# Dilated attention: relative bias added in PSUM by identity matmuls, exp read from PSUM

## Chip, cores and metric

The kernel runs on all 8 cores of one Trainium2 chip, one program on each. The time is device microseconds of the slowest core.

## What is computed

One decoder layer over 16384 positions of width 1024: forgetting attention (8 heads), dilated sliding-window attention (8 heads of 64), a cross-attention to 256 memory positions and a SwiGLU network. The part that matters here is the dilated attention. For each of three patterns (window, dilation), and within each residue class, a block of 128 queries sees its own block of 128 keys and the one before:

```python
DILATED_PATTERNS = ((128, 1), (512, 4), (2048, 16))
s = einsum('bhrnqd,bhrnkd->bhrnqk', qs, kk) * Dh ** -0.5      # blocks: 128 queries, 2 x 128 keys
s = s + bias                                                 # T5 bucket of the distance, per head
s = where(band & not_first, s, -inf)
o = softmax(s) @ vv ; lse = log of the denominator
# the three patterns are mixed with softmax(lse)
```

## The kernel before

Each core owns 2048 positions. It works in four stages with barriers between them: projections of the whole sequence (lines 395 to 497), forgetting attention (652 to 690), dilated attention (from 739), and everything after the attention (from 918). A small tracker records every instruction with the buffers that it reads and writes, in program order; each engine's queue is that order, and the waits are worked out from the buffers.

The dilated stage goes head by head. `c_loads(h)` loads Q, K, V and two bias tables of a head from HBM, on SyncE's queue (SP), into one of two sets; it is called a head ahead. BIC is 3 tables of 128 keys x 512 (the same 128 columns four times), for the current block, BIP 3 tables of 128 x 128 for the previous block; both hold -30000 where the band ends. Then V is transposed by TensorE in nine groups of up to 8 tiles (L854), each copied to VD by VectorE (L857); there is one PSUM bank for it, so matmuls and copies alternate. VD has ones in its columns 64 to 127, so that P.V yields the denominator too.

Twelve batches follow, four for each dilation 1, 4, 16. A batch is four items (query block, its key block, the previous key block). K, Q as matmul operands have 64 rows (head dimension); for d = 4 and d = 16 they are read in strides of 4 and 16 elements. A batch has three steps:

- s1: eight matmuls of 64 rows and 128 columns: four (L791) into one PSUM bank Sc_ps, four (L794) into another, Sp_ps
- s23: VectorE adds the tables, one L798 for Sc_ps and four L807 for Sp_ps, or L803 where the item reaches into the halo before the core's own positions and the mask HMASK is added too; ScalarE takes the exp of each (L809, L810)
- s45: eight matmuls of 128 rows and 128 columns (L815 and L817 in turn) multiply with VD into OD_ps; VectorE copies (L829) or adds (L831) that into ACCD

Sc_ps, Sp_ps and OD_ps have two banks each. The order is written out: s1 and s23 of the first two batches, then for each batch i its s45 followed by s1 and s23 of batch i + 2. A head ends with a reciprocal of the denominators (L871) and a multiply (L872), both on VectorE.

Of the kernel before, what the change touches and what calls it, by code (L numbers as in the profile page):

```python
# [6 lines left out]
F32 = mybir.dt.float32  # L7
BF16 = mybir.dt.bfloat16
AF = mybir.ActivationFunctionType
ALU = mybir.AluOpType  # L10
# [212 lines left out]
def build_program(debug=False):  # L223
    nc = bass.Bass("TRN2", target_bir_lowering=False)
    mk = MK(nc)
# [62 lines left out]
    with ExitStack() as st:  # L288
        ARENA_F = 49 * 1024
        arena_t = st.enter_context(nc.sbuf_tensor("arena", [128, ARENA_F], F32))  # L290
        ar = Arena(arena_t, ARENA_F)
# [3 lines left out]
        def B(name):  # L295
            return mk.buf(name)
# [4 lines left out]
        IDB = ar.alloc(128, BF16)  # L301
# [3 lines left out]
        HMASK = ar.alloc(1, F32)  # L305
# [3 lines left out]
        bC = B("consts")  # L309
# [7 lines left out]
        bC2 = B("consts2")  # L317
# [4 lines left out]
                                         op0=ALU.mult), reads=[bC], writes=[bC, bC2])  # L322
# [13 lines left out]
        for i in range(7):  # L336
            s = i % 2
            mk.dma(lambda e, i=i, s=s: e.dma_start(out=WST[s], in_=w_a_v[:, :, 440 * i:440 * (i + 1)]),
                   writes=[bWST[s]])
            for kc in range(8):  # L340
                if kc % 2 == 0:
                    mk.dve(lambda e, i=i, s=s, kc=kc: e.tensor_scalar(out=WA[:, kc, 440 * i:440 * (i + 1)], in0=WST[s][:, kc, :],
                                                                      scalar1=GPRE[:, 0, kc:kc + 1], scalar2=None, op0=ALU.mult),
                           reads=[bWST[s], bC], writes=[bWAc[i]])
                else:
                    mk.act(lambda e, i=i, s=s, kc=kc: e.activation(out=WA[:, kc, 440 * i:440 * (i + 1)], in_=WST[s][:, kc, :],
                                                                   func=AF.Copy, scale=GPRE[:, 0, kc:kc + 1]),
                           reads=[bWST[s], bC], writes=[bWAc[i]])
# [96 lines left out]
        for b in range(NBLK):  # L445
# [21 lines left out]
            for i in range(4):  # L467
# [3 lines left out]
                       reads=[bPR[k]], writes=[bVT[vs]])  # L471
# [4 lines left out]
            if b % 2 == 1:  # L476
                sb_ = b // 2
                mk.dma(lambda e, sb_=sb_: e.dma_start(out=V_v[:, :, 1024 * sb_:1024 * (sb_ + 1)],
                                                      in_=VST.rearrange("p h t d -> p h (t d)")),
                       reads=[bVST], writes=[DB("V", sb_)], eng="act")  # L480
            mk.act(lambda e, k=k: e.activation(out=GE[0:8, :], in_=PR_ps[k][0:8, :], func=AF.Exp,
                                               bias=NBF[0:8, :], scale=-1.0), reads=[bPR[k], bC2], writes=[bGE])
            mk.act(lambda e: e.activation(out=GSP[0:8, :], in_=GE[0:8, :], func=AF.Ln, bias=1.0, scale=1.0),
                   reads=[bGE], writes=[bGSP])
            cs = b % 2
            if b == 0:
                mk.dve(lambda e: e.tensor_tensor_scan(out=CS[0][0:8, :], data0=ONES8[0:8, :], data1=GSP[0:8, :],
                                                      initial=0.0, op0=ALU.mult, op1=ALU.add),
                       reads=[bGSP, bC2], writes=[bCS[0]])
            else:  # L490
                mk.dve(lambda e, cs=cs: e.tensor_tensor_scan(out=CS[cs][0:8, :], data0=ONES8[0:8, :],
                                                             data1=GSP[0:8, :], initial=CS[1 - cs][0:8, 511:512],
                                                             op0=ALU.mult, op1=ALU.add),
                       reads=[bGSP, bC2, bCS[1 - cs]], writes=[bCS[cs]])
            if b >= 28:
                ob = b - 28
                mk.dve(lambda e, cs=cs: e.tensor_scalar(out=NCS[0:8, :], in0=CS[cs][0:8, :], scalar1=-1.0, scalar2=None,
                                                        op0=ALU.mult), reads=[bCS[cs]], writes=[bNCS])
                mk.dma(lambda e, ob=ob: e.dma_start(out=C_s[:, 512 * ob:512 * (ob + 1)], in_=NCS[0:8, :]),
                       reads=[bNCS], writes=[DB("C", ob)], eng="act")  # L500
# [197 lines left out]
        for h in range(8):  # L698
            for ci in range(4):
                ulist = [(kt, p) for kt in range(32 * ci, 32 * ci + 32) for p in range(2) if kt <= last_kt(2 * p + 1)]  # L700
                units = {}
                n = len(ulist)
# [17 lines left out]
        DQT2 = [ar.alloc(OWN, BF16) for _ in range(2)]; bDQT2 = [B("DQT0"), B("DQT1")]  # L720
        DKT2 = [ar.alloc(2 * OWN, BF16) for _ in range(2)]; bDKT2 = [B("DKT0"), B("DKT1")]
        DVT2 = [ar.alloc(2 * OWN, BF16) for _ in range(2)]; bDVT2 = [B("DVT0"), B("DVT1")]
        BIC2 = [ar.alloc(3 * 512, F32).rearrange("p (b n) -> p b n", n=512) for _ in range(2)]; bBIC2 = [B("BIC0"), B("BIC1")]
        BIP2 = [ar.alloc(3 * 128, F32).rearrange("p (b n) -> p b n", n=128) for _ in range(2)]; bBIP2 = [B("BIP0"), B("BIP1")]
        VD = ar.alloc(69 * 128, BF16).rearrange("p (t d) -> p t d", d=128)
        bVD = B("VD")
        SC2 = [ar.alloc(512, F32) for _ in range(2)]; bSC2 = [B("SC0"), B("SC1")]
        SPv2 = [ar.alloc(512, F32) for _ in range(2)]; bSPv2 = [B("SPv0"), B("SPv1")]
        PC2 = [ar.alloc(512, BF16) for _ in range(2)]; bPC2 = [B("PC0"), B("PC1")]
        PP2 = [ar.alloc(512, BF16) for _ in range(2)]; bPP2 = [B("PP0"), B("PP1")]  # L730
        ACCD = ar.alloc(OWN, F32); bACCD = B("ACCD")
# [26 lines left out]
        def c_loads(h):  # L758
            z = h % 2
            mk.dma(lambda e: e.dma_start(out=DQT2[z][0:64, :], in_=DQ_s[h]), reads=allDQ, writes=[bDQT2[z]])  # L760
            mk.dma(lambda e: e.dma_start(out=DKT2[z][0:64, :], in_=DK_s[h]), reads=allDK, writes=[bDKT2[z]])
            mk.dma(lambda e: e.dma_start(out=DVT2[z][0:64, :], in_=DV_s[h]), reads=allDV, writes=[bDVT2[z]])
            mk.dma(lambda e: e.dma_start(out=BIC2[z], in_=dbiasc_d[h].rearrange("b p n -> p b n")), writes=[bBIC2[z]])
            mk.dma(lambda e: e.dma_start(out=BIP2[z], in_=dbiasp_d[h].rearrange("b p n -> p b n")), writes=[bBIP2[z]])

        def make_batch(h, bi, d, g, vidx):
            z = h % 2
            DQT, DKT, BIC, BIP = DQT2[z], DKT2[z], BIC2[z], BIP2[z]
            bDQT, bDKT, bBIC, bBIP = bDQT2[z], bDKT2[z], bBIC2[z], bBIP2[z]
            KV = kview(DKT[0:64, :], d)  # L770
            QV = qview(DQT[0:64, :], d)
            y = cst["n"] % 2
            cst["n"] += 1
            Sc_ps, bScp, Sp_ps, bSpp, OD_ps, bODp = Sc_ps2[y], bScp2[y], Sp_ps2[y], bSpp2[y], OD_ps2[y], bODp2[y]
            SC, bSC, SPv, bSPv, PC, bPC, PP, bPP = SC2[y], bSC2[y], SPv2[y], bSPv2[y], PC2[y], bPC2[y], PP2[y], bPP2[y]
            items = []
            for jj in range(4):
                if d == 1:
                    j = 4 * g + jj
                    items.append((QV[:, j, :], KV[:, 16 + j, :], KV[:, 15 + j, :], vidx[(1, 16 + j)], vidx[(1, 15 + j)], j == 0))  # L780
                elif d == 4:
                    m, r = g, jj
                    items.append((QV[:, m, r, :], KV[:, 4 + m, r, :], KV[:, 3 + m, r, :], vidx[(4, 4 + m, r)],
                                  vidx[(4, 3 + m, r)], m == 0))
                else:
                    r = 4 * g + jj
                    items.append((QV[:, r, :], KV[:, 1, r, :], KV[:, 0, r, :], vidx[(16, 1, r)], vidx[(16, 0, r)], True))

            def s1():
                for jj, it in enumerate(items):  # L790
                    mk.pe(lambda e, jj=jj, it=it: e.matmul(Sc_ps[:, 128 * jj:128 * (jj + 1)], it[1], it[0], start=True, stop=True),  # L791
                          reads=[bDKT, bDQT], writes=[bScp])
                for jj, it in enumerate(items):
                    mk.pe(lambda e, jj=jj, it=it: e.matmul(Sp_ps[:, 128 * jj:128 * (jj + 1)], it[2], it[0], start=True, stop=True),  # L794
                          reads=[bDKT, bDQT], writes=[bSpp])

            def s23():
                mk.dve(lambda e: e.tensor_tensor(out=SC, in0=Sc_ps, in1=BIC[:, bi, :], op=ALU.add),  # L798
                       reads=[bScp, bBIC], writes=[bSC])
                for jj, it in enumerate(items):  # L800
                    sl_ = slice(128 * jj, 128 * (jj + 1))
                    if it[5]:
                        mk.dve(lambda e, sl_=sl_: e.scalar_tensor_tensor(out=SPv[:, sl_], in0=Sp_ps[:, sl_], scalar=HMASK[:, 0:1],  # L803
                                                                        in1=BIP[:, bi, :], op0=ALU.add, op1=ALU.add),
                               reads=[bSpp, bBIP, bC], writes=[bSPv])
                    else:
                        mk.dve(lambda e, sl_=sl_: e.tensor_tensor(out=SPv[:, sl_], in0=Sp_ps[:, sl_], in1=BIP[:, bi, :], op=ALU.add),  # L807
                               reads=[bSpp, bBIP], writes=[bSPv])
                mk.act(lambda e: e.activation(out=PC, in_=SC, func=AF.Exp), reads=[bSC], writes=[bPC])  # L809
                mk.act(lambda e: e.activation(out=PP, in_=SPv, func=AF.Exp), reads=[bSPv], writes=[bPP])  # L810

            def s45():
                for jj, it in enumerate(items):
                    sl_ = slice(128 * jj, 128 * (jj + 1))
                    mk.pe(lambda e, sl_=sl_, it=it: e.matmul(OD_ps[:, sl_], VD[:, it[3], :], PC[:, sl_], start=True, stop=False),  # L815
                          reads=[bVD, bPC], writes=[bODp])
                    mk.pe(lambda e, sl_=sl_, it=it: e.matmul(OD_ps[:, sl_], VD[:, it[4], :], PP[:, sl_], start=False, stop=True),  # L817
                          reads=[bVD, bPP], writes=[bODp])
                if d == 1:
                    oap = ACCD[:, 512 * g:512 * (g + 1)]  # L820
                    iap = OD_ps[:, :]
                elif d == 4:
                    oap = ACCD[:, 512 * g:512 * (g + 1)].rearrange("p (i r) -> p r i", r=4)
                    iap = OD_ps[:, :].rearrange("p (r i) -> p r i", r=4)
                else:
                    oap = ACCD[:, :].rearrange("p (i r) -> p r i", r=16)[:, 4 * g:4 * g + 4, :]
                    iap = OD_ps[:, :].rearrange("p (r i) -> p r i", r=4)
                if d == 1:
                    mk.dve(lambda e: e.tensor_copy(out=oap, in_=iap), reads=[bODp], writes=[bACCD])  # L829
                else:  # L830
                    mk.dve(lambda e: e.tensor_tensor(out=oap, in0=oap, in1=iap, op=ALU.add), reads=[bODp, bACCD], writes=[bACCD])  # L831
            return (s1, s23, s45)

        c_loads(0)
        for h in range(8):
            z = h % 2
# [408 lines left out]
```

How the kernel before makes its waits and increments, by code:

```python
                def body(eng):  # L168
# [2 lines left out]
                    def wait(sem, val):  # L171
                        kid = id(sem)
                        if known.get(kid, 0) >= val:
                            return
                        known[kid] = val
                        eng.wait_ge(sem, val)
# [10 lines left out]
                                wait(d.key.sem, d.key.inc_amt * dv)  # L187
                            else:
                                wait(esem[d.eng][d.sigval[0]], d.sigval[1])
                        ins = o.fn(eng)
                        if o.is_dma:
                            ins.then_inc(o.key.sem, o.key.inc_amt)
                        elif o.needs_signal:
                            ins.then_inc(esem[o.eng][o.sigval[0]], 1)
                    if ename == "sp":
                        for (k, v) in fin:
                            eng.wait_ge(k.sem, v)
```

## Time and profile before

| | |
|---|---|
| runs shown | 4790.36 and 4900.81 us, median 4845.58 us |
| the profiled execution | 4801.83 us, span of its slowest core (core 3) 4799.6 us |
| spans of the 8 cores | 4758.5 to 4799.6 us |
| busy, share of the span | TensorE (PE) 78%, weight loads (PEld) 31%, VectorE (DVE) 27%, ScalarE (ACT) 58%, GpSimd (POOL) 12% |
| mean granted TensorE clock, core 3 | 0.883 |

A profile comes from one execution and shows its slowest core. A busy time is the sum of an engine's instructions; matmuls overlap one another, so the distance from one start to the next tells their rate, not the duration of one. PEclk is the share of the full TensorE clock of 2.4 GHz that was granted. In a timeline, neighbours of the same line and shape are merged into one row with their count; a PE row is matmuls, a PEld row weight loads. An arrow with a name tells what an engine waited for.

### The profile page before, as it was taken

The page shows a single profiled execution, that of the slowest core. Times are in us where ns is not written, and L with a number is a line of the kernel's source. Part 1 is how long each engine was busy: PE and PEld are TensorE (multiplying, and loading weights), DVE is VectorE, ACT ScalarE, POOL GpSimd, SP SyncE. Part 2 cuts the span into 40 slices and gives each one's busy share as a digit, 9 for nine tenths or more (in the row PEclk, how much of TensorE's full clock was granted, in tenths as well). Part 3 has the DMA queues.
Part 4 walks back from the last instruction along what each step waited for, and adds up shares of the span by engine and source line. Part 5 has one row for each costly group of instructions (what it writes and reads, how often), then busy time and mean ns, then how long its engine had stood idle before and what let it go on. Part 6 is the DMA issues. An engine that isn't in the chain of part 4 may idle for free.

```text
span 4799.6 us, 63084 instructions; the slowest of 8 cores (4758.5 to 4799.6 us)
## 1 busy us (share of the span) xinstructions
PE 3751.5 (78%) x16856; PEld 1487.3 (31%) x16856; DVE 1281.0 (27%) x1945; ACT 2799.0 (58%) x3379; POOL 578.5 (12%) x509
## 2 busy tenths in 40 slices
PE   1787888892999999999999999995555437676767
PEld 0333333331333333333333333333333213232333
DVE  1332331114101020111111111007778432333321
ACT  2222222231999999999999999992222235353521
POOL 2333332200010002011120303200000000000000
PEclk9998999996999999999999999995555559898988
DMA  5455453222021112122221312202110302524245
GB/s 169 138 157 147 125 162 110 93 85 76 28 76 29 48 29 68 45 63 64 60 82 47 95 34 82 86 1 58 39 39 20 106 0 75 159 77 160 75 157 163
DMA packets 236377, 399.33 MB, mean 83 GB/s; under 512 B 16712, under 2 KB 110152, under 8 KB 228840
## 3 DMA queue, kind: packets, MB, share of 16 engines
q1 hardware_dynamic: 187072, 332.30, 23.2%
q10 hardware_dynamic: 48960, 63.00, 4.0%
q8 instruction: 147, 2.41, 0.2%
q14 instruction: 198, 1.62, 0.1%
HBM read 302.37 MB, written 92.86 MB: 82 GB/s over the span
## 4 chain that ended last, share of the span: by engine, by line
PE 51%; ACT 21%; DVE 12%; DMA 8%; issue 6%; ACTq 1%; SPq 0%; POOL 0%; DVEq 0%; POOLq 0%
PE psall L652 15%; ACT arena L667 14%; PE psall L677 11%; PE psall L395 10%; DMA KT_s<-arena 4%; PE psall L1131 2%; PE psall L1116 2%; DVE arena L871 2%; PE psall L1111 2%; ACT arena L935 2%; PE psall L1037 1%; DVE arena L960 1%; DVE arena L688 1%; ACT arena L810 1%; DVE arena L803 1%
## 5 line engine op out<-in xcount | busy, mean ns | idle before, releaser
L667 ACT ACTIVATE arena<-psall,arena 128x1024 bf16<-128x1024 f32 (+1 forms) x1984 | 1988.9, 1102 | 167.9 <-PE psall L652 155.1
L652 PE MATMUL psall<-arena 128*128 128x512 bf16 x3904 | 1172.2, 378 | 139.7 <-DVE arena L628 86.9
L677 PE MATMUL psall<-arena 128*128 128x512 bf16 x3904 | 1168.3, 379 | 29.0 <-DVE arena L690 15.6
L395 PE MATMUL psall<-arena 128*128 128x512 bf16 (+1 forms) x3072 | 729.9, 395 | 18.0 <-ACT arena L403 18.0
L652 PEld LDWEIGHTS psall<-arena 128*128 128x128 bf16 x3904 | 264.3, 96 | 995.9 <-issue 967.8
L677 PEld LDWEIGHTS psall<-arena 128*128 128x128 bf16 x3904 | 372.6, 96 | 516.4 <-issue 68.2
L688 DVE RECIPROCAL arena<-psall 64x512 f32<-64x512 f32 x32 | 107.5, 3359 | 1271.4 <-PE psall L677 1271.2
L395 PEld LDWEIGHTS psall<-arena 128*128 128x128 bf16 (+1 forms) x3072 | 299.1, 100 | 386.4 <-issue 75.1
L403 ACT ACTIVATE arena<-psall 128x512 bf16<-128x512 f32 x224 | 133.7, 597 | 332.3 <-PE psall L395 251.7
L599 POOL TENSOR_SCALAR arena<-arena 128x128 bf16<-128x128 f32 x352 | 212.0, 602 | 571.8 <-DMA arena<-w_gate 271.0
L809 ACT ACTIVATE arena<-arena 128x512 bf16<-128x512 f32 x96 | 60.7, 632 | 319.6 <-PE psall L794 240.0
L470 ACT ACTIVATE arena<-psall 128x512 bf16<-128x512 f32 x128 | 74.6, 597 | 274.3 <-PE psall L459 154.5
L416 POOL TENSOR_TENSOR arena<-arena 128x4096 bf16<-128x4096 f32 x32 | 224.4, 7013 | 68.8 <-DMA arena<-xT 68.8
L1131 PE MATMUL psall<-arena 128*128 128x512 bf16 x704 | 165.4, 392 | 71.9 <-DMA arena<-Wd_b 65.2
L1111 PE MATMUL psall<-arena 128*128 128x512 bf16 x704 | 179.7, 401 | 49.6 <-DMA arena<-Wg_b 48.3
L425 DVE TENSOR_TENSOR arena<-arena 128x512 bf16<-128x512 f32 x192 | 132.9, 692 | 291.1 <-PE psall L395 97.1
L935 ACT ACTIVATE arena<-psall 128x512 bf16<-128x512 f32 x96 | 57.4, 598 | 247.0 <-PE psall L1131 92.0
L1116 PE MATMUL psall<-arena 128*128 128x512 bf16 x704 | 181.9, 405 | 0.0
L854 PE MATMUL psall<-arena 64*128 64x64 bf16 x552 | 43.9, 239 | 175.2 <-DVE arena L857 158.9
L425 POOL TENSOR_TENSOR arena<-arena 128x512 bf16<-128x512 f32 x64 | 80.9, 1264 | 631.0 <-DVE arena L425 554.7
L617 DVE CAST arena<-arena 3x512 bf16<-3x512 f32 x32 | 13.4, 418 | 532.1 <-DMA arena<-C_s 529.7
L463 DVE COPY arena<-psall 128x512 bf16<-128x512 bf16 x128 | 54.3, 425 | 376.0 <-PE psall L459 358.6
(104 smaller groups left out, 2847.4 us busy)
## 6 DMA issues: line engine op xcount, KB each, us to landing
arena<-xT SPq DMA_DIRECT2D x32, 2048.0 KB, 10.6
arena<-Wd_b SPq DMA_DIRECT2D x176, 256.0 KB, 3.5
V_s<-arena ACTq DMA_DIRECT2D x16, 2048.0 KB, 10.2
arena<-V_s SPq DMA_DIRECT2D x32, 1024.0 KB, 6.8
arena<-Wg_b SPq DMA_DIRECT2D x88, 256.0 KB, 2.6
arena<-Wu_b SPq DMA_DIRECT2D x88, 256.0 KB, 2.6
KT_s<-arena ACTq DMA_DIRECT2D x128, 128.0 KB, 1.8
arena<-KT_s SPq DMA_DIRECT2D x32, 512.0 KB, 5.2
```

The lines of the kernel that those rows point to most:

```text
L395: mk.pe(lambda e, kc=kc, k=k: e.matmul(PR_ps[k][0:M, :], WA[:, kc, col0:col0 + M], HT[hs][:, kc, :], start=(kc == 0), stop=(kc == 7)), rea ...
L416: mk.pool(lambda e: e.tensor_tensor(out=XSQ, in0=XT[xs], in1=XT[xs], op=ALU.mult), reads=[bXT[xs]], writes=[bXSQ])
L425: fn = (lambda e, kc=kc: e.tensor_tensor(out=HT[hs][:, kc, :], in0=XT[xs][:, kc, :], in1=RSTD, op=ALU.mult))
L599: mk.pool(lambda e, wb=wb, stg=stg, gi_=gi_, kc_=kc_: e.tensor_scalar(out=wb[:, 128 * kc_:128 * (kc_ + 1)], in0=stg[:, 128 * kc_:128 * (kc ...
L652: mk.pe(lambda e, qb=qb, col=col, diag=diag: e.matmul(SP2[sl][:, col:col + 512], KR[ci][:, 128 * kl:128 * (kl + 1)], QTp[:, 512 * qb:512 * ...
L667: mk.act(lambda e: e.activation(out=PT[ps][:, c0:c1], in_=SP2[sl][:, c0:c1], func=AF.Exp, bias=negc_all[:, kt, h:h + 1], scale=1.0), reads ...
L677: mk.pe(lambda e, qb=qb, col=col: e.matmul(O_ps[qb], VR[ci][:, kl, :], PT[ps][:, col:col + 512], start=(kt == 0), stop=(kt == last_kt(qb)) ...
L688: mk.dve(lambda e, qb=qb, r=r: e.reciprocal(out=RCPf[r][0:64, :], in_=O_ps[qb][64:128, :]), reads=[bOp[qb]], writes=[bRCPf[r]])
L935: mk.act(lambda e, iap=iap, col=col, n=n, off=off: e.activation(out=SQJ[:, off:off + n], in_=iap, func=AF.Square, accum_out=SSd[:, col:col ...
L1111: mk.pe(lambda e, kc=kc, wg=wg, y=y: e.matmul(G_ps2[y], WC[wg][:, 128 * kc:128 * (kc + 1)], HTd[:, kc, :], start=(kc == 0), stop=(kc == 7) ...
L1116: mk.pe(lambda e, kc=kc, wu=wu, y=y: e.matmul(U_ps2[y], WC[wu][:, 128 * kc:128 * (kc + 1)], HTd[:, kc, :], start=(kc == 0), stop=(kc == 7) ...
L1131: mk.pe(lambda e, t=t, tt=tt, j=j, hh=hh, wd=wd: e.matmul(PSB[2 * tt + hh], ATt[:, j, 128 * t:128 * (t + 1)], WC[wd][:, 512 * hh:512 * (hh ...
```

## The change

Bias tables are cast to bf16 on VectorE after they are loaded, two casts in each `c_loads` (only the first 128 columns of BIC). In s1, every Q.K matmul is followed by a matmul of the 128 x 128 identity IDB with the table, which accumulates into the same 128 columns of PSUM. The VectorE adds are gone, and ScalarE's exp reads Sc_ps and Sp_ps directly. HMASK becomes the bias operand of the exp; the exp is split in two in the one batch of a head where only the first item reaches into the halo.

```diff
         BIP2 = [ar.alloc(3 * 128, F32).rearrange("p (b n) -> p b n", n=128) for _ in range(2)]; bBIP2 = [B("BIP0"), B("BIP1")]
         VD = ar.alloc(69 * 128, BF16).rearrange("p (t d) -> p t d", d=128)
         bVD = B("VD")
-        SC2 = [ar.alloc(512, F32) for _ in range(2)]; bSC2 = [B("SC0"), B("SC1")]
-        SPv2 = [ar.alloc(512, F32) for _ in range(2)]; bSPv2 = [B("SPv0"), B("SPv1")]
+        BICb2 = [ar.alloc(3 * 128, BF16).rearrange("p (b n) -> p b n", n=128) for _ in range(2)]; bBICb2 = [B("BICb0"), B("BICb1")]
+        BIPb2 = [ar.alloc(3 * 128, BF16).rearrange("p (b n) -> p b n", n=128) for _ in range(2)]; bBIPb2 = [B("BIPb0"), B("BIPb1")]
         PC2 = [ar.alloc(512, BF16) for _ in range(2)]; bPC2 = [B("PC0"), B("PC1")]
         PP2 = [ar.alloc(512, BF16) for _ in range(2)]; bPP2 = [B("PP0"), B("PP1")]
         ACCD = ar.alloc(OWN, F32); bACCD = B("ACCD")
@@ -762,17 +762,19 @@
             mk.dma(lambda e: e.dma_start(out=DVT2[z][0:64, :], in_=DV_s[h]), reads=allDV, writes=[bDVT2[z]])
             mk.dma(lambda e: e.dma_start(out=BIC2[z], in_=dbiasc_d[h].rearrange("b p n -> p b n")), writes=[bBIC2[z]])
             mk.dma(lambda e: e.dma_start(out=BIP2[z], in_=dbiasp_d[h].rearrange("b p n -> p b n")), writes=[bBIP2[z]])
+            mk.dve(lambda e: e.tensor_copy(out=BICb2[z], in_=BIC2[z][:, :, 0:128]), reads=[bBIC2[z]], writes=[bBICb2[z]])
+            mk.dve(lambda e: e.tensor_copy(out=BIPb2[z], in_=BIP2[z]), reads=[bBIP2[z]], writes=[bBIPb2[z]])
 
         def make_batch(h, bi, d, g, vidx):
             z = h % 2
-            DQT, DKT, BIC, BIP = DQT2[z], DKT2[z], BIC2[z], BIP2[z]
-            bDQT, bDKT, bBIC, bBIP = bDQT2[z], bDKT2[z], bBIC2[z], bBIP2[z]
+            DQT, DKT, BICb, BIPb = DQT2[z], DKT2[z], BICb2[z], BIPb2[z]
+            bDQT, bDKT, bBICb, bBIPb = bDQT2[z], bDKT2[z], bBICb2[z], bBIPb2[z]
             KV = kview(DKT[0:64, :], d)
             QV = qview(DQT[0:64, :], d)
             y = cst["n"] % 2
             cst["n"] += 1
             Sc_ps, bScp, Sp_ps, bSpp, OD_ps, bODp = Sc_ps2[y], bScp2[y], Sp_ps2[y], bSpp2[y], OD_ps2[y], bODp2[y]
-            SC, bSC, SPv, bSPv, PC, bPC, PP, bPP = SC2[y], bSC2[y], SPv2[y], bSPv2[y], PC2[y], bPC2[y], PP2[y], bPP2[y]
+            PC, bPC, PP, bPP = PC2[y], bPC2[y], PP2[y], bPP2[y]
             items = []
             for jj in range(4):
                 if d == 1:
@@ -788,26 +790,32 @@
 
             def s1():
                 for jj, it in enumerate(items):
-                    mk.pe(lambda e, jj=jj, it=it: e.matmul(Sc_ps[:, 128 * jj:128 * (jj + 1)], it[1], it[0], start=True, stop=True),
+                    sl_ = slice(128 * jj, 128 * (jj + 1))
+                    mk.pe(lambda e, sl_=sl_, it=it: e.matmul(Sc_ps[:, sl_], it[1], it[0], start=True, stop=False),
                           reads=[bDKT, bDQT], writes=[bScp])
-                for jj, it in enumerate(items):
-                    mk.pe(lambda e, jj=jj, it=it: e.matmul(Sp_ps[:, 128 * jj:128 * (jj + 1)], it[2], it[0], start=True, stop=True),
-                          reads=[bDKT, bDQT], writes=[bSpp])
-
-            def s23():
-                mk.dve(lambda e: e.tensor_tensor(out=SC, in0=Sc_ps, in1=BIC[:, bi, :], op=ALU.add),
-                       reads=[bScp, bBIC], writes=[bSC])
+                    mk.pe(lambda e, sl_=sl_: e.matmul(Sc_ps[:, sl_], IDB, BICb[:, bi, :], start=False, stop=True),
+                          reads=[bC2, bBICb], writes=[bScp])
                 for jj, it in enumerate(items):
                     sl_ = slice(128 * jj, 128 * (jj + 1))
-                    if it[5]:
-                        mk.dve(lambda e, sl_=sl_: e.scalar_tensor_tensor(out=SPv[:, sl_], in0=Sp_ps[:, sl_], scalar=HMASK[:, 0:1],
-                                                                        in1=BIP[:, bi, :], op0=ALU.add, op1=ALU.add),
-                               reads=[bSpp, bBIP, bC], writes=[bSPv])
-                    else:
-                        mk.dve(lambda e, sl_=sl_: e.tensor_tensor(out=SPv[:, sl_], in0=Sp_ps[:, sl_], in1=BIP[:, bi, :], op=ALU.add),
-                               reads=[bSpp, bBIP], writes=[bSPv])
-                mk.act(lambda e: e.activation(out=PC, in_=SC, func=AF.Exp), reads=[bSC], writes=[bPC])
-                mk.act(lambda e: e.activation(out=PP, in_=SPv, func=AF.Exp), reads=[bSPv], writes=[bPP])
+                    mk.pe(lambda e, sl_=sl_, it=it: e.matmul(Sp_ps[:, sl_], it[2], it[0], start=True, stop=False),
+                          reads=[bDKT, bDQT], writes=[bSpp])
+                    mk.pe(lambda e, sl_=sl_: e.matmul(Sp_ps[:, sl_], IDB, BIPb[:, bi, :], start=False, stop=True),
+                          reads=[bC2, bBIPb], writes=[bSpp])
+
+            def s23():
+                mk.act(lambda e: e.activation(out=PC, in_=Sc_ps, func=AF.Exp), reads=[bScp], writes=[bPC])
+                halo = [it[5] for it in items]
+                if all(halo):
+                    mk.act(lambda e: e.activation(out=PP, in_=Sp_ps, func=AF.Exp, bias=HMASK[:, 0:1], scale=1.0),
+                           reads=[bSpp, bC], writes=[bPP])
+                elif not any(halo):
+                    mk.act(lambda e: e.activation(out=PP, in_=Sp_ps, func=AF.Exp), reads=[bSpp], writes=[bPP])
+                else:
+                    assert halo == [True, False, False, False]
+                    mk.act(lambda e: e.activation(out=PP[:, 0:128], in_=Sp_ps[:, 0:128], func=AF.Exp, bias=HMASK[:, 0:1], scale=1.0),
+                           reads=[bSpp, bC], writes=[bPP])
+                    mk.act(lambda e: e.activation(out=PP[:, 128:512], in_=Sp_ps[:, 128:512], func=AF.Exp),
+                           reads=[bSpp], writes=[bPP])
 
             def s45():
                 for jj, it in enumerate(items):
```

## Rows read from the trace of the kernel before

**Rows 1.** Window of the dilated stage: busy us of PE, PEld, DVE, ACT, POOL; PEclk, DMA, GB/s.

```profile
3280.00:3779.00 499.00, 274.05 (x2038) 191.93 (x2035) 401.68 (x658) 121.31 (x192) 0.00 (x0) 0.50 0.12 30
```

**Rows 2.** Groups by line and shape, 3262 to 3780 us: busy us, mean ns | idle before.

```profile
L871 DVE RECIPROCAL arena<-arena 64x2048 f32<-64x2048 f32 x8 | 103.6, 12947 | 0.8
...
L831 DVE TENSOR_TENSOR arena<-arena,psall 128x512 f32<-128x512 f32 x64 | 67.7, 1058 | 9.1 <-PE psall L854 5.7 <-PE psall L817 3.4
L798 DVE TENSOR_TENSOR arena<-psall,arena 128x512 f32<-128x512 f32 x96 | 65.4, 681 | 1.5 <-PE psall L794 0.9 <-PE psall L791 0.3 <-PE psall L815 0.2
L807 DVE TENSOR_TENSOR arena<-psall,arena 128x128 f32<-128x128 f32 x216 | 62.4, 289 | 17.9 <-DVE arena L807 0.6
L809 ACT ACTIVATE arena<-arena 128x512 bf16<-128x512 f32 x96 | 60.7, 632 | 319.6 <-PE psall L794 240.0 <-PE psall L817 58.7 <-PE psall L815 15.6
...
L803 DVE SCALAR_TENSOR_TENSOR arena<-psall,arena 128x128 f32<-128x128 f32 x168 | 58.4, 348 | 12.5
```

**Rows 3.** Timeline of the dilated stage: start us, duration us, engine line operation.

```profile
3272.33 0.42 DVE L857 COPY arena<-psall 128x512 bf16<-128x512 bf16 x1 [0.92 <-PE psall L854]
...
3637.55 12.95 DVE L871 RECIPROCAL arena<-arena 64x2048 f32<-64x2048 f32 x1
...
3663.40 0.61 PE L791 MATMUL psall<-arena 64*128 64x128 bf16 x4
...
3669.22 0.68 DVE L798 TENSOR_TENSOR arena<-psall,arena 128x512 f32<-128x512 f32 x1
...
3671.79 0.68 DVE L798 TENSOR_TENSOR arena<-psall,arena 128x512 f32<-128x512 f32 x1
...
3701.16 12.95 DVE L871 RECIPROCAL arena<-arena 64x2048 f32<-64x2048 f32 x1
```

**Rows 4.** Timeline of TensorE, end and start of s45 around s1, d = 4.

```profile
3741.45 0.31 PE L815 MATMUL psall<-arena 128*128 128x128 bf16 x1
3741.55 0.31 PE L817 MATMUL psall<-arena 128*128 128x128 bf16 x1
...
3741.80 0.35 PEld L791 LDWEIGHTS psall<-arena 64*128 64x128 bf16 x4 [0.20 <-issue]
...
3741.80 0.64 PE L791 MATMUL psall<-arena 64*128 64x128 bf16 x4
3742.26 0.64 PE L794 MATMUL psall<-arena 64*128 64x128 bf16 x4
3742.83 0.10 PEld L815 LDWEIGHTS psall<-arena 128*128 128x128 bf16 x1 [0.21 <-issue]
3742.84 0.29 PE L815 MATMUL psall<-arena 128*128 128x128 bf16 x1
```

**Rows 5.** Timeline of TensorE, the same for d = 16.

```profile
3755.22 0.41 PE L794 MATMUL psall<-arena 64*128 64x128 bf16 x1
3755.56 0.29 PE L815 MATMUL psall<-arena 128*128 128x128 bf16 x1
...
3756.76 1.16 PE L791 MATMUL psall<-arena 64*128 64x128 bf16 x4
```

**Rows 6.** Timeline of TensorE at granted clock 1.00, last stage.

```profile
4047.75 0.59 PE L1111 MATMUL psall<-arena 128*128 128x512 bf16 x2
4048.28 0.39 PE L1060 MATMUL psall<-arena 64*128 64x512 bf16 x1
4048.59 0.60 PE L1116 MATMUL psall<-arena 128*128 128x512 bf16 x2
```

**Rows 7.** Load of BIP, line L764: the second one, its landing, and that of the third.

```profile
L764 SPq DMA_DIRECT2D arena<-dbiasp x1: 1234/1234/1234, 3267.6 to 3267.6; - x1
...
DMA to landing us min/median/max: 15.6/15.6/15.6
...
DMA to landing us min/median/max: 8.1/8.1/8.1
```

**Rows 8.** Groups by line and shape, VectorE casts.

```profile
L547 DVE CAST arena<-arena 128x512 bf16<-128x512 f32 x4 | 1.7, 427 | 16.3 <-DMA arena<-negm 16.3
```

## Prediction

> **What bounds the kernel now.** I read the windows by stage first; that of the dilated attention, the only stage that the change touches, is shown [rows 1]. It holds 499 of 4800 us, all but the loads at the stage's start. VectorE is busy 402 of them, TensorE 274, ScalarE 121, and the granted clock is 0.50, the lower of TensorE's two levels (1.2 GHz), throughout. So whatever the edit gives or takes, it does so inside about 500 us.
>
> Next the groups by line and shape [rows 2]: the bias adds of L798, L803 and L807 hold VectorE for 65 + 58 + 62 = 186 us, the sums into ACCD (L831) for 68, the reciprocals (L871) for 104. Then the order in time of one head [rows 3]. One head lasts 63.6 us, from reciprocal to reciprocal (3637.55 to 3701.16). Of these the twelve batches take 37.8 us, from the first L791 at 3663.40 to the next reciprocal; the other 26 are the reciprocal, its multiply and the transposes of V, in which the change adds only two casts. Within the batches VectorE runs one instruction after the other: two L798 of neighbouring batches start 2.57 us apart, which is 0.68 + 4 x 0.37 + 0.68 less their overlaps. So the batches are bound by VectorE, and the adds are what it mostly does there. That speaks for the change.
>
> But TensorE isn't far behind: its 16 matmuls a batch start over 0.1 us apart [rows 4], which makes 1.7 of 2.57 us. So the question is what 8 more of them in each batch cost there.
>
> **What is removed.** Per batch one L798 and four L803 or L807, about 0.68 + 4 x 0.32 = 2 us of VectorE; what stays is one sum of 0.7 to 1.06 us. VectorE then no longer sets the pace. The exps read PSUM in place of SBUF. I price them at the 0.63 us of L809 [rows 2]; two of them, 1.26 us, hide beside TensorE as long as a batch takes over some 1.5 us, and would still hide at twice that in what follows. The one batch per head whose exp is split in two adds one short ScalarE instruction, hidden for the same reason.
>
> **What is added to TensorE.** s1 issues Q.K and identity matmuls alternately: 8 of 64 rows and 8 of 128 rows, 16 changes of row count a batch. Now s1 has eight of 64 rows in a run and s45 eight of 128 in a run, two changes a batch. What a change costs can be read [rows 4]. Inside the run of L815 and L817 the starts are 0.105 us apart (3741.45, 3741.55; 128 columns at the lower clock). From the last L817 to the first L791, 128 to 64 rows, it is 0.25 (3741.80), and the weight load of L791 starts only there too. From L791 to L794, both of 64 rows but in another bank, four starts take 0.46, that is 0.115 each, with no gap. From the last L794 (the group of four starts at 3742.26 and lasts 0.64, one lasts 0.29, so the last starts at 3742.61) to L815, 64 to 128 rows, it is 0.23. Where Q and K are read in strides of 16 (d = 16) [rows 5], four L791 take 1.16 us with a last one of 0.42, so 0.245 apart, and from an L794 at 3755.22 to the L815 at 3755.56 it is 0.34. At the full clock the same is there [rows 6]: the start after the second L1111 would come 0.215 us later within a run of 512 columns, and L1060 with its 64 rows comes at 4048.28, 0.315 after it; back to 128 rows takes 0.31 again. So a change of row count costs some 0.10 to 0.14 us, about a weight load (0.10, L815 in [rows 4]) that otherwise hides behind the matmul before. Waits aren't what it costs: L794 has waits of its own too, as its bank must be free of the adds of L803 and L807, and shows no gap.
>
> The Trainium skill, page "TensorEngine Tiling (Array Packing)", section Tiling Modes, says that changing the tiling mode drains TensorE. The rows above agree, and put its price at 0.10 to 0.14 us. This is a rule against the change as it is ordered.
>
> Whether an identity matmul alone between two of 64 rows pays as much as the ends of runs do, the trace doesn't show. Lower bound: stream and load, 0.107 + 0.10 = 0.21 each way (0.33 out of a strided one). Upper bound: 0.25 each way, 0.37 out of a strided one. I take the measured ones, 0.22 and 0.24, as nearest: a pair of Q.K and identity costs 0.46 us, for d = 16 it costs 0.34 + 0.24 = 0.58.
>
> **The sum.** A batch for d = 1 or 4: 8 x 0.46 = 3.68, less 0.13 since the last identity is followed by L815 with 128 rows too, plus s45's 7 x 0.107 + 0.24 = 0.99: 4.54 us. For d = 16: 4.64 - 0.13 + 0.99 = 5.50 us. Twelve batches: 8 x 4.54 + 4 x 5.50 = 58.3, and 1.6 from the last matmul to the reciprocal (its end, the last sum of L831): 59.9 us against 37.8. That is +22.1 a head, +177 us for eight heads. By the lower bounds the batches are 4.22 and 5.2 us and eight heads cost +147; by the upper ones 4.86 and 5.82, and +208. TensorE has no other wait in this: after s1 of a batch comes s45 of the batch two before, whose exps had a whole batch of over 4 us.
>
> Casts: two of 128 x 384 to bf16 a head. L547 casts 128 x 512 in 0.43 us [rows 8], so 0.35 each by size. They stand on VectorE between the multiply of one head (L872) and the first copy of the next (L857), and TensorE's transposes wait for those copies, so their 0.7 us are on the path: 8 x 0.7 = 6 us. In VectorE's order they also wait for the loads of the next head's tables. SP issues these when the last Q.K of the head before is done. The load of BIP took 15.6 us to land in the crowd at the start [rows 7]; later there are 13 us of reciprocal and 2.3 of multiply before the casts, and the loads have been in by then (two later ones took some 8), so no wait there. But for head 0, the tables of head 1, issued at 3267.6, land at 3283.2, where the first copy now runs at 3272.33 [rows 7, 3]: with everything behind it on VectorE it comes 11 us later, and the casts of head 0 are under that. Once 12 us. SP's own queue gains nothing and loses nothing: the table loads stand behind DQ and DK, which wait for the matmuls.
>
> Total: 177 + 6 + 12 = +195 us on the profiled execution of 4801.83 us (span 4799.6): **4997 us**, 4.1% slower. The two runs shown were 4790 and 4901, with a median of 4846, so the profiled one is near the faster of them, and 4997 is the time beside that.
>
> **Rivals.** (1) Changing the row count costs nothing of its own, and the two gaps a batch come from something at the ends of s1 and s45. Then every added matmul costs 0.107: batches of 24 x 0.107 + 0.25 = 2.82, 2.89 for d = 4, and 8 x (0.245 + 0.107) + 0.86 + 0.25 = 3.93 for d = 16: 38.6 + 1.6 = 40.2 a head, +2.4, with casts +37 us: 4839. TensorE takes over as the bound just where VectorE leaves it. Against it stand the gapless L791 to L794, and [rows 6], where neither s1 nor s45 is in play. The Trainium skill, page "TensorE: Matmul & The Clock Gate", Part 2, says that a weight load is pulled ahead of running matmuls when the row groups don't conflict or when it goes to the background buffer; by that the identity's load could hide and this rival would hold. The trace shows the pull only between equal row counts.
>
> (2) As (1), and the denser stream brings the clock to its upper level. Then 128 columns take 0.054 (a quarter of the 0.215 of [rows 6]): 24 x 0.054 + 0.2 = 1.5 for d = 1 and 4, with ScalarE's 1.26 just under it, and 8 x (0.245 + 0.054) + 0.43 + 0.2 = 3.0 for d = 16 if the strided read doesn't gain: 24 + 1.6 = 25.6 a head, -12.2, less 97 plus 18: 4723, not slower. It decides itself at the row count's price and at the clock.
>
> (3) The changes of row count cost what I say, but the clock rises: pairs of 0.15 + 0.16 and batches of 2.9 (4.4 for d = 16): 42.5 a head, +56 us in all: 4858. Against (2) and (3): the clock is 0.50 over 499 us now, with columns moving in 16 x 0.107 of a 2.57 us batch, 67% of the time. Mine has 24 x 0.107 of 4.54, 57%, so it is less dense than what now stays at the lower level. That the change doesn't take place is no issue; each edit is an instruction.
>
> **Chances.** The forecast 0.84, (1) 0.06, (2) 0.03, (3) 0.05, others 0.02: that the strided read, too, takes half its time under (2), 8 x 0.12 less in each batch of d = 16 and 31 us less in all, 4692, over 2% faster. Its own bounds are 4802 + 147 + 18 = 4967 and 4802 + 208 + 18 = 5028; the spread of the runs shown is added, mostly upward, and a little below for a smaller lone-identity price: 4930 to 5070. About 2% is what a measurement of this kernel can tell from no change. Slower 0.85, for the forecast and for times of (3) above its middle; same 0.13, faster 0.02.
>
> **What will show it.** In the changed profile: heads of 86 us between reciprocals; a clock of 0.50; matmuls of 64 and 128 rows alternating 0.2 to 0.25 us apart with the weight load starting with its own matmul, not before; TensorE the bound of the batches, VectorE busy under 30% in them; the first copy of the stage near 3284. I am wrong if pairs are 0.21 us apart (rival 1) or the clock is at 1 in the batches (2, 3).

## The result and the profile after

The changed kernel takes 4995.78 us (median of 11 runs, 4965 to 5104); the kernel before 4808.55 (10 runs, 4790 to 4901). The ratio is 1.0384, 95% interval 1.0354 to 1.0413: slower, by 187 us in the medians. Medians are of all runs, while every ratio here leaves out the runs in which four cores or all eight were granted a lower clock than usual and took longer (of the changed kernel, five of the 11, at 5032 to 5104 us). The profiled execution has a span of 4988.9 us on its slowest core, core 4, which is 189 more than the span of before.

The dilated stage of the changed kernel, as one window of core 4, with the columns of [rows 1]:

```profile
3298.80:3970.00 671.20, 495.84 (x2783) 275.85 (x2783) 242.32 (x187) 120.31 (x200) 0.00 (x0) 0.50 0.09 21
```

The eight heads' window was 499 us in [rows 1] and is 671 now. VectorE fell from 402 to 242 us, so the change does what it says. TensorE rose from 274 to 496, and the clock is still 0.50. One head's batches, seen alone:

```profile
3896.70:3955.60 58.90, 57.46 (x291) 30.66 (x289) 11.77 (x13) 15.04 (x25) 0.00 (x0) 0.50 0.00 1
```

TensorE is busy 57.5 of 58.9 us, VectorE 11.8 (20%). The groups by line and shape, as in [rows 2]:

```profile
L794 PE MATMUL psall<-arena 64*128 64x128 bf16 x384 | 129.2, 336 | 0.0
L800 PE MATMUL psall<-arena 64*128 64x128 bf16 x384 | 129.1, 336 | 0.0
L796 PE MATMUL psall<-arena 128*128 128x128 bf16 x384 | 110.8, 288 | 0.0
L802 PE MATMUL psall<-arena 128*128 128x128 bf16 x384 | 110.8, 288 | 0.0
L879 DVE RECIPROCAL arena<-arena 64x2048 f32<-64x2048 f32 x8 | 103.6, 12948 | 0.8
...
L839 DVE TENSOR_TENSOR arena<-arena,psall 128x512 f32<-128x512 f32 x64 | 69.3, 1082 | 225.9 <-PE psall L825 194.6 <-PE psall L823 30.5
...
L806 ACT ACTIVATE arena<-psall 128x512 bf16<-128x512 f32 x96 | 57.3, 597 | 441.5 <-PE psall L796 439.2 <-PE psall L800 2.3
```

L796 and L802 are the identities. The adds have no row any more; the sum into ACCD (now L839) is as long as L831 was, but waits 226 us for TensorE where it waited 9. The exp waits for the identities. Everything stands in line behind TensorE. The timeline of TensorE, matmuls (PE) with some of their weight loads (PEld), first for d = 1 and then for d = 16, shows why, beside [rows 4, 5]:

```profile
3904.56 0.29 PE L794 MATMUL psall<-arena 64*128 64x128 bf16 x1
3904.78 0.29 PE L796 MATMUL psall<-arena 128*128 128x128 bf16 x1
3904.99 0.10 PEld L794 LDWEIGHTS psall<-arena 64*128 64x128 bf16 x1
3905.00 0.29 PE L794 MATMUL psall<-arena 64*128 64x128 bf16 x1
3905.21 0.10 PEld L796 LDWEIGHTS psall<-arena 128*128 128x128 bf16 x1
3905.22 0.29 PE L796 MATMUL psall<-arena 128*128 128x128 bf16 x1
...
3908.93 0.29 PE L794 MATMUL psall<-arena 64*128 64x128 bf16 x1
...
3944.97 0.43 PE L800 MATMUL psall<-arena 64*128 64x128 bf16 x1
3945.33 0.29 PE L802 MATMUL psall<-arena 128*128 128x128 bf16 x1
3945.55 0.43 PE L800 MATMUL psall<-arena 64*128 64x128 bf16 x1
3945.92 0.29 PE L802 MATMUL psall<-arena 128*128 128x128 bf16 x1
...
3946.59 0.31 PE L823 MATMUL psall<-arena 128*128 128x128 bf16 x1
3946.59 0.15 PEld L825 LDWEIGHTS psall<-arena 128*128 128x128 bf16 x1
3946.69 0.31 PE L825 MATMUL psall<-arena 128*128 128x128 bf16 x1
```

Each matmul of s1 starts 0.22 us after the one before, and its weight load starts only 0.01 us before it. The runs of s45 keep 0.105 us, and there the load starts a whole step ahead: that of L825 at 3946.59, with the matmul before its own. A pair takes 0.44 us (3904.56 to 3905.00), for d = 16 it takes 0.58 (3944.97 to 3945.55), and a batch for d = 1 takes 4.37 (3904.56 to 3908.93). VectorE, over the start of the stage and over two heads, beside [rows 3]:

```profile
3286.59 0.55 DVE L765 CAST arena<-arena 128x384 bf16<-128x384 f32 x1 [8.16 <-DMA arena<-dbiasc]
3287.10 0.36 DVE L766 CAST arena<-arena 128x384 bf16<-128x384 f32 x1
3287.38 0.42 DVE L865 COPY arena<-psall 128x512 bf16<-128x512 bf16 x1
...
3870.93 12.95 DVE L879 RECIPROCAL arena<-arena 64x2048 f32<-64x2048 f32 x1
...
3955.68 12.95 DVE L879 RECIPROCAL arena<-arena 64x2048 f32<-64x2048 f32 x1
```

From the first Q.K of the last head (3896.66) to its reciprocal it is 59.0 us; before it was 37.8. VectorE's wait of 8.2 us for a table of head 1 is there. The first copy comes 18.8 us after VectorE begins its memset of VD, in place of 8.3.

The 187 us, from the traces of the slowest cores: batches 8 x (58.99 - 37.65) = 170.7; the rest of a head 26.56 in place of 25.82, 7 x 0.74 = 5; the first copy 10.5. Together 186.4, and from the memset of VD to the last reciprocal the stage is 687.1 us in place of 500.5, 186.6 more. I read the experiments in the same two measures, the batches of a head (first matmul of s1 to the reciprocal, mean over the heads) and the whole time, because the stages before this one alone differ by up to 77 us between the cores of one run.

### The profile page after: what moved, and what is told of

The parts are those of the page before. It is cut to its first block, busy times and chain, and to the rows that moved or that the text cites. A ratio compares the mean times of both kernels' runs of the same rounds, so it can differ in the third digit from the quotient of the medians.

```text
span 4988.9 us, 62608 instructions; the slowest of 8 cores (4927.2 to 4988.9 us)
## 1 busy us (share of the span) xinstructions
PE 3975.5 (80%) x17624; PEld 1573.9 (32%) x17624; DVE 1124.0 (23%) x1481; ACT 2795.2 (56%) x3387; POOL 578.5 (12%) x509
## 4 chain that ended last, share of the span: by engine, by line
PE 56%; ACT 19%; DVE 10%; DMA 8%; issue 5%; ACTq 1%; SPq 0%; POOL 0%; DVEq 0%; POOLq 0%
PE psall L652 14%; ACT arena L667 13%; PE psall L677 11%; PE psall L395 10%; DMA KT_s<-arena 4%; PE psall L1139 3%; PE psall L1124 2%; DVE arena L879 2%; PE psall L800 2%; PE psall L794 2%; PE psall L1119 2%; PE psall L796 2%; PE psall L802 2%; ACT arena L943 2%; PE psall L1045 1%
## 5 line engine op out<-in xcount | busy, mean ns | idle before, releaser
L652 PE MATMUL psall<-arena 128*128 128x512 bf16 x3904 | 1174.5, 379 | 137.9 <-DVE arena L628 85.0
L677 PE MATMUL psall<-arena 128*128 128x512 bf16 x3904 | 1170.5, 380 | 29.0 <-DVE arena L690 15.7
L403 ACT ACTIVATE arena<-psall 128x512 bf16<-128x512 f32 x224 | 133.6, 596 | 336.2 <-PE psall L395 252.0
L806 ACT ACTIVATE arena<-psall 128x512 bf16<-128x512 f32 x96 | 57.3, 597 | 441.5 <-PE psall L796 439.2
L470 ACT ACTIVATE arena<-psall 128x512 bf16<-128x512 f32 x128 | 74.5, 596 | 270.2 <-PE psall L459 155.6
L1139 PE MATMUL psall<-arena 128*128 128x512 bf16 x704 | 166.5, 395 | 67.6 <-DMA arena<-Wd_b 60.7
L1119 PE MATMUL psall<-arena 128*128 128x512 bf16 x704 | 178.9, 400 | 47.1 <-DMA arena<-Wg_b 45.9
L943 ACT ACTIVATE arena<-psall 128x512 bf16<-128x512 f32 x96 | 57.3, 597 | 248.8 <-PE psall L1139 90.4
L1124 PE MATMUL psall<-arena 128*128 128x512 bf16 x704 | 181.4, 404 | 0.0
L459 PE MATMUL psall<-arena 128*128 128x128 bf16 x512 | 55.0, 236 | 127.9 <-ACT arena L470 103.9
L419 PE MATMUL psall<-arena 128*128 128x512 bf16 x256 | 63.8, 394 | 102.4 <-POOL arena L416 102.4
```

The lines of the kernel that those rows point to most:

```text
L403: mk.act(lambda e: e.activation(out=EST[s], in_=PR_ps[k], func=AF.Copy, scale=scale), reads=[bPR[k]], writes=[bEST[s]])
L652: mk.pe(lambda e, qb=qb, col=col, diag=diag: e.matmul(SP2[sl][:, col:col + 512], KR[ci][:, 128 * kl:128 * (kl + 1)], QTp[:, 512 * qb:512 * ...
L677: mk.pe(lambda e, qb=qb, col=col: e.matmul(O_ps[qb], VR[ci][:, kl, :], PT[ps][:, col:col + 512], start=(kt == 0), stop=(kt == last_kt(qb)) ...
L943: mk.act(lambda e, iap=iap, col=col, n=n, off=off: e.activation(out=SQJ[:, off:off + n], in_=iap, func=AF.Square, accum_out=SSd[:, col:col ...
L1119: mk.pe(lambda e, kc=kc, wg=wg, y=y: e.matmul(G_ps2[y], WC[wg][:, 128 * kc:128 * (kc + 1)], HTd[:, kc, :], start=(kc == 0), stop=(kc == 7) ...
L1124: mk.pe(lambda e, kc=kc, wu=wu, y=y: e.matmul(U_ps2[y], WC[wu][:, 128 * kc:128 * (kc + 1)], HTd[:, kc, :], start=(kc == 0), stop=(kc == 7) ...
```

## The experiments

The diffs are excerpts; three dots stand for what is left out.

**Q.K matmuls of 128 rows.** Nothing but the row count: same order, same number.

```diff
+        for t_ in DQT2 + DKT2:
+            mk.pool(lambda e, t_=t_: e.memset(t_[64:128, :], 0.0), writes=[bHI])
...
-            KV = kview(DKT[0:64, :], d)
-            QV = qview(DQT[0:64, :], d)
+            KV = kview(DKT, d)
+            QV = qview(DQT, d)
...
```

> The changed kernel with nothing altered but the row count of the Q.K matmuls: 128 rows, rows 64 to 127 of Q and K being zeros set once, the order and number of all matmuls as in the changed kernel. My theory (each change of row count costs about 0.115 us, 16 of them a batch): no change is left, pairs are 0.107 us apart per matmul, and the batches of a head fall from 58.9 us by 12 x 16 x 0.115 = 22 to about 37 us, the time from 4996 to about 4820, if the clock stays at 0.50; the stream is then without gaps and denser than anything in this stage, so the clock may rise, and then the batches take about 26 us and the time is about 4740. Rival (it is the number of added matmuls, whatever their rows): about 4996, and pairs stay 0.44 us apart.

Measured: 4777.69 us, ratio to the kernel before 0.990 (0.981 to 0.998). Batches 28.0 us, 31 less than in the changed kernel. The batches of one head and the stretch that follows them, core 2 (windows):

```profile
3325.00:3353.00 28.00, 25.89 (x286) 21.89 (x283) 12.06 (x13) 14.52 (x25) 0.00 (x0) 0.92 0.09 21
3353.00:3380.00 27.00, 5.39 (x67) 4.55 (x68) 19.08 (x13) 0.00 (x0) 0.00 (x0) 0.51 0.27 65
```

So the rows of two operands, with zeros in them, take 218 us off the kernel. Two things happened at once: the gaps are gone, and the clock is 0.92 over the batches, falling back to 0.50 between the batches of one head and those of the next. The next two runs separate them.

**Four changes of row count a batch, and two.** The same 24 matmuls with 64 and 128 rows, in another order: four identities and then four Q.K for Sc_ps, and the same for Sp_ps. The first identity of a bank starts its accumulation.

```diff
+                for jj in range(4):
+                    sl_ = slice(128 * jj, 128 * (jj + 1))
+                    mk.pe(lambda e, sl_=sl_, jj=jj: e.matmul(Sc_ps[:, sl_], IDB, BICb[:, bi, :], start=(jj == 0), stop=False),
...
-                    mk.pe(lambda e, sl_=sl_, it=it: e.matmul(Sc_ps[:, sl_], it[1], it[0], start=True, stop=False),
+                    mk.pe(lambda e, sl_=sl_, it=it, jj=jj: e.matmul(Sc_ps[:, sl_], it[1], it[0], start=False, stop=(jj == 3)),
...
```

With two changes, both banks' identities come before both banks' Q.K.

> The same 24 matmuls a batch with 64 and 128 rows as in the changed kernel, ordered in s1 as four identities, four Q.K, four identities, four Q.K: four changes of row count a batch in place of 16. My theory: 12 changes fewer, 12 x 0.115 = 1.4 us a batch, 16.6 us a head, batches of a head 42 us, time about 4863. Rival (number of matmuls): about 4996.

> The same 24 matmuls, ordered in s1 as eight identities, then eight Q.K: two changes of row count a batch, as in the kernel before. My theory: 14 changes fewer, 19.3 us a head, batches of a head 39.6 us, time about 4842 with the clock at 0.50; a good deal less if the clock rises. It should stand 20 us under the run with four changes. Rival (number of matmuls): about 4996.

Measured with four: 4868.56 us, ratio 1.010 (1.005 to 1.016), batches 42.4 to 42.5 us on all eight cores. With two: 4807.78 us, ratio 0.997 (0.995 to 1.000), batches 35.0 us on the core shown, 33.9 to 34.8 on the others. Batches of one head with four changes (core 3) and with two (core 4), in windows:

```profile
3844.80:3887.20 42.40, 40.91 (x289) 27.84 (x288) 11.61 (x13) 15.07 (x25) 0.00 (x0) 0.50 0.00 1
```

```profile
3732.60:3768.70 36.10, 34.50 (x289) 26.61 (x288) 11.78 (x13) 14.17 (x25) 0.00 (x0) 0.64 0.01 2
```

With four changes the clock is 0.50 all through, as in the changed kernel, and there are 144 changes fewer in a head's twelve batches: (58.9 - 42.5) / 144 = 0.114 us each, with number and shape of the matmuls and the clock all the same. With two changes 19.3 us were expected at the same clock and 24.0 came, with the clock at 0.64 or 0.70 in every head of the core shown, and at 0.82 in a few heads of others. A batch of the run with four, TensorE's timeline, from one s45 to the next (runs merged; L794 and L802 are the identities):

```profile
3849.09 0.29 PE L827 MATMUL psall<-arena 128*128 128x128 bf16 x1
...
3849.91 0.63 PE L794 MATMUL psall<-arena 128*128 128x128 bf16 x4
3850.48 0.61 PE L798 MATMUL psall<-arena 64*128 64x128 bf16 x4
3851.02 0.61 PE L802 MATMUL psall<-arena 128*128 128x128 bf16 x4
3851.56 0.60 PE L806 MATMUL psall<-arena 64*128 64x128 bf16 x4
3852.10 0.29 PE L827 MATMUL psall<-arena 128*128 128x128 bf16 x1
```

The first run of four takes 0.57 us, each other 0.54: three steps of 0.107 and one of 0.22. The batch takes 3.01 us in place of 4.37, 0.113 for each of the 12 changes that are gone.

**Control: the kernel before with 128 rows.** The same edit as in the first run, made to the kernel before.

> Control: the kernel before with Q.K matmuls of 128 rows (zeros below), so without its two changes of row count a batch. VectorE is the bound of its batches, so my theory gives no difference that can be measured, within 10 us of the kernel before. If it gains 20 us or more, TensorE was a bound of the batches beside VectorE, and my account of the kernel before is wrong.

Measured: 4830.12 us, ratio 1.001 (0.998 to 1.004), batches 37.7 us as before. In 29 of the 64 heads (eight heads on each of eight cores) the mean clock of the batches is 0.54 or 0.55, where the kernel before has 0.50 in all 64, and the batches are no shorter for it. So neither the two changes of row count nor TensorE's clock cost the kernel before anything, and VectorE alone was its bound.

**Identity of 64 rows.** It leaves out the bias of keys 64 to 127, and keeps everything else that could be blamed: alternation, two sources of weights, 24 matmuls, accumulation.

```diff
-                    mk.pe(lambda e, sl_=sl_: e.matmul(Sc_ps[:, sl_], IDB, BICb[:, bi, :], start=False, stop=True),
+                    mk.pe(lambda e, sl_=sl_: e.matmul(Sc_ps[:, sl_], IDB[0:64, :], BICb[0:64, bi, :], start=False, stop=True),
...
```

> The changed kernel, its order and its 24 matmuls a batch, but the identity matmuls use rows 0 to 63 only, so that all sixteen matmuls of s1 have 64 rows and the row count changes twice a batch. Left out: the bias of keys 64 to 127 of each block. My theory (the change of row count is what costs): 14 changes fewer at 0.114 us, batches of a head 39.7 us, time about 4845; the weight loads hide though identity and Q.K still alternate and each loads its own weights. Rival (alternating identity and Q.K, two sources of weights, is what keeps the load from hiding): batches stay 58.9 us, time 4996.

Measured: 4840.03 us, ratio 1.004 (1.001 to 1.008), batches 38.5 us. One batch, TensorE's timeline, and that head's window:

```profile
3768.84 0.29 PE L823 MATMUL psall<-arena 128*128 128x128 bf16 x1
...
3769.56 0.31 PE L825 MATMUL psall<-arena 128*128 128x128 bf16 x1
3769.81 0.28 PE L794 MATMUL psall<-arena 64*128 64x128 bf16 x1
3769.89 0.31 PE L796 MATMUL psall<-arena 64*128 64x128 bf16 x1
3769.99 0.31 PE L794 MATMUL psall<-arena 64*128 64x128 bf16 x1
...
3771.38 0.31 PE L802 MATMUL psall<-arena 64*128 64x128 bf16 x1
3771.62 0.29 PE L823 MATMUL psall<-arena 128*128 128x128 bf16 x1
```

```profile
3765.30:3803.80 38.50, 36.92 (x292) 29.45 (x289) 11.77 (x13) 14.96 (x25) 0.00 (x0) 0.50 0.01 1
```

Identity and Q.K alternate 0.1 us apart, and the only gaps are the steps where the row count changes, 0.25 us from 3769.56 to 3769.81 and 0.24 to 3771.62. The batch takes 2.78 us in place of 4.37, 0.114 for each of the 14 changes that are gone. The clock is 0.50. Alternation isn't what costs. The batches came out 1.2 us under the 39.7 expected. In this order the strides cost less: a batch for d = 4 takes 2.79 us like one for d = 1, and for d = 16 it takes 3.67, where the steps of before, read from runs of Q.K, gave 3.93 (rival 1).

**The casts on GpSimd.** `mk.dve` becomes `mk.pool` in the two added lines of c_loads, alone and together with 128 rows.

> The changed kernel with its two casts a head on GpSimd in place of VectorE. My account of the small terms: the first copy of V no longer waits for head 1's tables (10 us once) and eight heads lose 0.7 us each, so 16 us less, about 4980 and a first copy near 3277 or 10 us earlier than now. Rival (the casts were hidden, or GpSimd is late with them): no difference, or slower.

> Q.K matmuls of 128 rows as in the first experiment, and the casts on GpSimd. If both terms are as I say they add up: batches 28.0 us a head, heads 54.6 - 0.7, and 10 us less once: about 4750, which is 1.2% to 1.4% under the kernel before. If the heads don't get shorter the casts were not on the path.

Alone: 4986.69 us, ratio 1.035 (1.030 to 1.039), 9 us less in the whole time, which isn't clear of its noise; the stage from memset to last reciprocal is shorter by 15 to 17 us on every core (670.9 in place of 687.1, median of the cores), of it 11 at the first copy. The two terms were real and together of the forecast size. With 128 rows: 4735.45 us, ratio 0.983 (0.979 to 0.987). The stage falls from 440 to 429 us, not by the full 16: the batches rose from 28.0 to 28.5 us. Why wasn't followed up.

**Q in the order of its reads.** The run before, 128 rows and casts on GpSimd, and for d = 4 and 16 the Q.K matmuls read copies of Q, which VectorE makes once a head.

```diff
+            for d_ in (4, 16):
...
+                mk.dve(lambda e, o_=o_, d_=d_, z=z: e.tensor_copy(out=o_, in_=qview(DQT2[z][0:64, :], d_)),
+                       reads=[bDQT2[z]], writes=[bQC[d_]])
...
```

> As the run with 128 rows and casts on GpSimd, and Q for d = 4 and d = 16 is first copied by VectorE into the order in which the matmuls read it, so that their moving operand is contiguous. At the full clock the strided d = 16 matmuls are 0.213 us apart in place of 0.056: 8 x 0.157 = 1.25 us a batch, four batches a head, 5 us, and about 1 us for d = 4. Batches 22 us a head if TensorE is their bound, bounded below by ScalarE's 12 x 1.1 us; time about 4705. If the strided weight load (K) is what makes them slow, nothing changes.

Measured: 4704.83 us (4668 to 4814), ratio 0.972 (0.967 to 0.978), the fastest of all. Batches 20.6 us on six cores, 1.4 under the 22 expected: a batch for d = 4 fell from 1.83 to 1.34 us, twice what was taken, and one for d = 16 from 2.77 to 1.41. The rest of a head stayed at 25.96 us, so the copies of Q don't show. In the run of 128 rows without it, for d = 16 (first fence, core 2), and with it (second fence), at the upper clock:

```profile
3727.05 0.40 PE L797 MATMUL psall<-arena 128*128 128x128 bf16 x1
3727.26 0.24 PE L799 MATMUL psall<-arena 128*128 128x128 bf16 x1
3727.34 0.39 PE L797 MATMUL psall<-arena 128*128 128x128 bf16 x1
```

```profile
3400.57 0.23 PE L803 MATMUL psall<-arena 128*128 128x128 bf16 x1
3400.63 0.22 PE L805 MATMUL psall<-arena 128*128 128x128 bf16 x1
3400.69 0.23 PE L803 MATMUL psall<-arena 128*128 128x128 bf16 x1
```

A pair takes 0.29 us with a strided Q and 0.12 without, though K is still strided.

## Why the prediction was right

The bound was read right: VectorE in the batches, TensorE close behind. The control shows that TensorE's two gaps a batch cost nothing while VectorE led, and the window of after that TensorE leads now.

The price of a change of row count, the step on which all rests, is confirmed three ways: fewer changes with the same matmuls (0.114 us each), none with zero rows, and alternation at equal row count without gaps. By the trace of before it was 0.10 to 0.14. What fills those 0.11 us isn't separated: I had called it about a weight load that otherwise hides, but at a change the load itself starts only 0.21 us after the matmul before, where in a run it starts with it, so the gap on record lies ahead of the load. Whether the array empties first, or the load takes the time and is recorded late, no run tells. The identity alone between two matmuls of 64 rows, which that trace didn't show, pays it like the end of a run: 0.22 to each side. I had taken 0.22 and 0.24, so my batches of d = 1 are 0.17 us too long (4.54 against 4.37), those of d = 16 right (5.50 against 5.52; eight pairs of 0.58). Batches of a head: 59.9 forecast, 59.0 measured.

The terms: batches +177 forecast, +171 measured; casts on the path 6 and 5; the first copy's wait 12 and 10.5. The sum was 195, the stage grew by 186.6. A cast takes 0.55 and 0.36 us, not 0.35 twice, but they overlap and 0.74 us a head is what they cost. That the forecast of 4997 lies 1 us from the measured median is luck: it was made on the profiled execution at 4802, the profiled execution of after took 4990, 7 less than forecast, and the sum is 8 too large.

Rival 1 (no price, 2.82 us a batch) and rival 2 (no price, and the upper clock, 4723) fell with the gaps. But rival 2 is what the run with 128 rows became, with batches of 28.0 us where I had worked out 25.6. On the core shown the first 4 to 6 us of each head's batches ran at 0.50 (0.92 over all of them), and a batch for d = 4 took 1.83 us where I had 1.5, one for d = 16 2.77 where I had 3.0. Rival 3 (price and upper clock) fell, the clock stayed at 0.50. My reason for it, that this stream is less dense than the one of before, doesn't settle it: the run with the identity of 64 rows has matmuls 0.107 us apart with two gaps a batch, far denser than either, and stayed at 0.50 as well.

The Trainium skill, page "TensorEngine Tiling (Array Packing)", section Tiling Modes, says that a change of tiling mode drains TensorE. The traces agree so far as no step between 64 and 128 rows in this stage is under 0.19 us (kernels before and after, four changes, identity of 64 rows); the price is 0.114 us at the lower clock. The Trainium skill, page "TensorE: Matmul & The Clock Gate", Part 2, says that a weight load is pulled ahead of running matmuls when it goes to the background buffer. In the four traces just named a load starts 0.105 us ahead of its matmul (median) between matmuls of equal row count, and at most 0.03 us ahead, mostly 0.004, between 64 and 128 rows.

## What to carry to other kernels

Before moving work to TensorE, look up in the trace what happens where its matmuls change from 64 to 128 rows: here each change cost 0.11 us, as much as a matmul of 128 columns itself. Group matmuls by row count, or fill the short ones up with rows of zeros, which cost no time here; the same fold of the bias then made the kernel 1.0% faster than before in place of 3.8% slower, 1.7% with the casts on GpSimd, and 2.8% with the moving operand contiguous too; only the last is clear of the 2% taken as the bar in the prediction. That gain came with the clock: at 0.50 and with two changes a batch (the identity of 64 rows) the batches took 38.5 us, no less than the 37.7 of before. And an engine that is 67% busy beside the bound isn't a free place for half as much work again.

## What the hardware showed unexpectedly

With rows of zeros the clock rose. The same 24 matmuls a batch ran at a granted clock of 0.50 with 16 changes, with 4, and with all of s1 at 64 rows without a gap inside it; at 0.64 to 0.82, by the head, with eight identities of 128 rows in a run next to s45's; and at 0.92 when every matmul had 128 rows. In the last, what TensorE did before the rise was matmuls of 128 rows back to back; with 64 rows in s1, back to back too, no rise came in any head of any core. The control shows the same with 16 matmuls a batch: the same zeros brought 29 of 64 heads to 0.54 or 0.55.

A moving operand read in strides of 16 elements (32 bytes) takes 0.245 us for 128 columns at the lower clock [rows 5], and 0.21 at the upper one (3727.05 to 3727.26), where a contiguous one takes 0.105 and 0.06. It hardly gains from the clock. Strides of 4 elements take 0.115 at the lower clock [rows 4]; at the upper one, in the run with 128 rows, a pair of Q.K and identity takes 0.17 to 0.18 (3717.86 to 3718.03, core 2), where two contiguous ones take 0.11. Weights in strides of 16 cost little: in the fastest kernel, with Q contiguous for every d, a batch for d = 16 takes 1.41 us and one for d = 1 1.34.

In the profiled execution of the fastest kernel two cores, 0 and 1, had most of their upper stretches in this stage at a granted clock of 0.81, with batches of 22.0 and 21.9 us in place of 20.6; window of core 1:

```profile
3366.00:3386.00 20.00, 17.74 (x269) 17.24 (x266) 13.36 (x14) 12.75 (x22) 0.00 (x0) 0.81 0.20 41
```

Core 2 was granted 0.99 over its own (3391 to 3408). The 0.81 is a level between 0.50 and 1.00, and no run was made to find its cause.
